# The expert products of the first block, reordered: eight by the high weights, then four by the low weights behind a wait of their own

## The reference, cut to what matters

```
logits = u @ router_w + router_b ; top 4 of 32 experts per token, softmax gates
for each block of gathered token rows xb of an expert e:
    gu  = xb @ w_gu[e] + b_gu[e]                    # 1024 -> 2048
    act = (clip(up) + 1) * gate * sigmoid(1.702 * gate)
    out = act @ w_down[e] + b_down[e]               # 1024 -> 1024
h += gate-weighted sum of the experts' outputs ; final RMSNorm
```

## Time and profile before

| what | value |
|---|---|
| time, median of 3 runs | 2208.36 us (2207.04 to 2212.03) |
| the profiled execution, its own time | 2210.34 us |
| its span, first to last instruction | 2208.3 us |
| mean granted TensorE clock over the span | 0.978 |
| expert stage, about | 650 to 2180 us of the span |

### The profile page before, as it was taken

How to read it: one execution, slowest core, us unless ns; L and a number is a source line. 1 busy time by engine, 2 the same in 40 slices (tenths; PEclk the granted TensorE clock), 3 DMA queues, 4 the chain that set the end, 5 groups by cost and what they waited for, 6 DMA issues and landing times. The chain is left out here.

```text
span 2208.3 us, 35903 instructions
## 1 busy us (share of the span) xinstructions
PE 2133.2 (97%) x11230; PEld 1811.5 (82%) x11231; DVE 1706.5 (77%) x2127; ACT 1373.6 (62%) x1752; POOL 408.2 (18%) x436
## 2 busy tenths in 40 slices
PE   7999999988959999999999999999999999999998
PEld 7987777767848998898898898988889998889884
DVE  5426667776658777979979978779997778998897
ACT  4324655544447566757857757567775667776675
POOL 0000000002342121213213213212321222221120
PEclk9999999999969999999999999999999999999996
DMA  4111101207859776979979979669997769998897
GB/s 162 44 48 34 58 34 44 101 31 229 181 185 343 248 241 248 377 265 349 382 263 353 377 259 352 236 243 380 373 382 267 252 229 332 388 364 336 290 370 283
DMA packets 106797, 548.41 MB, mean 248 GB/s; under 512 B 18071, under 2 KB 28824, under 8 KB 51834
## 3 DMA queue, kind: packets, MB, share of 16 engines
q1 hardware_dynamic: 88138, 504.89, 61.2%
q0 software_dynamic: 18608, 42.85, 8.1%
HBM read 516.45 MB, written 41.47 MB: 253 GB/s over the span
## 5 line engine op out<-in xcount | busy, mean ns | idle before, releaser
L2431 DVE TENSOR_TENSOR wl<-raw,wh 128x2048 fp32r<-128x2048 f32 x423 | 959.1, 2287 | 44.0 <-PE sums L2188 26.8
L2292 ACT ACTIVATE wh<-raw 128x2048 fp32r<-128x2048 f32 x425 | 804.7, 1912 | 113.2 <-PE sums L2188 39.4
L2172 PE MATMUL sums<-wh,xx 128*128 128x512 f32 x832 | 325.8, 392 | 0.9 <-issue 0.9
L2171 PE MATMUL sums<-wl,xx 128*128 128x512 f32 x832 | 325.6, 391 | 0.0
L2170 PE MATMUL sums<-wh,xx 128*128 128x512 f32 x832 | 325.3, 391 | 0.0
L2103 POOL DMA_INDIRECT h_dram<-y,pairs_mine x47 | 120.8, 2570 | 769.1 <-DVE y L2525 449.2
L2170 PE MATMUL sums<-wh,al 128*128 128x512 f32 x560 | 226.7, 405 | 0.6 <-DVE al L2516 0.3
L2172 PE MATMUL sums<-wh,ah 128*128 128x512 f32 x560 | 219.1, 391 | 0.0
L2171 PE MATMUL sums<-wl,ah 128*128 128x512 f32 x560 | 218.5, 390 | 0.0
L2171 PEld LDWEIGHTS sums<-wl,xx 128*128 128x128 f32 x832 | 156.9, 189 | 34.0
L2172 PEld LDWEIGHTS sums<-wh,xx 128*128 128x128 f32 x832 | 156.7, 188 | 33.4
(11 more groups left out here) (402 smaller groups left out, 4174.6 us busy)
## 6 DMA issues: line engine op xcount, KB each, us to landing
raw<-in_w_experts SPq DMA_DIRECT2D x426, 1024.0 KB, 6.5
raw<-in_w_chan SPq DMA_DIRECT2D x20, 512.0 KB, 3.3
o_gate<-in_x SPq DMA_DIRECT2D x8, 512.0 KB, 5.9
raw<-in_w_out SPq DMA_DIRECT2D x8, 512.0 KB, 5.5
ht<-in_x SPq DMA_DIRECT2D x8, 512.0 KB, 5.9
h_dram<-ht SPq DMA_DIRECT2D x8, 512.0 KB, 9.0
u_dram<-ut SPq DMA_DIRECT2D x8, 512.0 KB, 10.1
h_all<-h_dram SPq DMA_DIRECT2D x8, 512.0 KB, 6.8
```

The lines of the kernel that those rows point to most:

```text
L2171: pe.matmul(out, hi[:, n, :], w_lo[:, kk, :], start=False, stop=False)
L2172: last = pe.matmul(out, hi[:, n, :], w_hi[:, kk, :], start=False, stop=half == 1 and kk == 3)
L2292: nc.scalar.activation(wh[ch % HIGHS][:, :, :], raw[ch % RAW][:, :, :], ACT.Copy).then_inc(h_split.sem, 1)
L2431: dve.tensor_tensor(wl[ch % LOWS][:, :, :], raw[ch % RAW][:, :, :], wh[ch % HIGHS][:, :, :], ALU.subtract).then_inc(l_split.sem, 1)
```

## The change

Only `first_block` changes. Before, the chunk waits for its low weights and runs, for each of its four tiles, the three matmuls in turn. After, it waits at its head for its high weights only, runs the two matmuls by the high weights of all four tiles (eight in all), waits for its low weights, and runs the four matmuls by the low weights. The wait for the activations stays in the first loop, in front of tiles n = 4 and n = 6 of chunk 10. The number of matmuls, their operands and the chunk's last signal stay.

```
     def first_block(i, ch):
         g, half = GROUP_OF[ch], HALF_OF[ch]
-        pe.wait_ge(*low_done(i, ch))
+        pe.wait_ge(h_split.sem, h_split.at(i, ch + 1))
...
             if ch == LAST_CHUNK[4] and n % 2 == 0:
                 pe.wait_ge(a_low.sem, a_low.at(i, n // 2 + 1))
             pe.matmul(out, lo[:, n, :], w_hi[:, kk, :], start=g >= 4 and n == 0, stop=False)
-            pe.matmul(out, hi[:, n, :], w_lo[:, kk, :], start=False, stop=False)
-            last = pe.matmul(out, hi[:, n, :], w_hi[:, kk, :], start=False, stop=half == 1 and kk == 3)
+            pe.matmul(out, hi[:, n, :], w_hi[:, kk, :], start=False, stop=False)
+        pe.wait_ge(*low_done(i, ch))
+        for kk in range(4):
+            n = half * 4 + kk
+            last = pe.matmul(out, hi[:, n, :], w_lo[:, kk, :], start=False, stop=half == 1 and kk == 3)
         return last
```

## The result

Over 22 runs of each kernel the median went from 2209.74 us (2205.71 to 2212.03) to 2211.37 us (2209.21 to 2217.18). The ratio is 1.0014, with a 95% interval from 1.0008 to 1.0020: 3.1 us slower (1.8 to 4.4). The two medians are only 1.6 us apart; the means, 2209.29 and 2212.36 us, are 3.1 apart, because five of the runs after lie above 2214 us and none of those before does. It is slower, but within the 0.2% that the prediction called no change; forecast were 6.2 us.

What follows compares the result with a forecast made beforehand. PE was taken to bound the kernel, busy for 1491.5 of 1495 us of the expert stage. Chunk 10's stalls of 4.6, 0.4 and 1.2 us sum to 6.2, so 2208.4 becomes 2214.6 us, range 2209.3 to 2218.3.

Steps and rivals of the forecast that it cites:

- Starting on the high weights gains nothing.: At the head of each chunk: the wait for low weights never held PE, so moving it back gains 0 us.
- The added waits and the operand order are free.: In all 348 `first_block` calls: one more satisfied wait and another operand order, both taken as 0 us.
- the 3.5 us at the top of the range: Upper bound for the 348 added waits at 0.01 us each; a little of it was put into the range's top.
- The fourth pair is due two products earlier, and a typical single item loses 0.27 us.: Chunk 10, single items: the fourth activation pair is awaited before product five, not seven; 17 items lose 0.27 us each.
- The item that the sum took at 0.43: One single item whose fourth pair in chunk 10 is 0.16 us later than in the typical ones; loss 0.43 us.
- The five late items.: Five single items where chunk 10's load already waited for `al` before, 2.5 us in total; forecast to add 1.2 us.
- A wait in the chain is a wait of the whole stage, since PE has no idle time later in which to make it good.: Expert stage: PE's stalls in chunk 10 were counted in full towards the kernel's time, 6.2 us.
- the likeliest case: The stall in chunk 10, chance 0.72: 6.2 us slower, 2214.6 us.
- the case in which nothing measurable happens: Rival, chance 0.18: PE's loads run far enough ahead, or something else paces the item; 2208.4 us, give or take 1.
- The step of 216 ns: The skill's spacing of 512-column matmuls, against 226 to 230 ns in the rows; would make the sum about 0.6 us smaller.
- The rival of something else being the pacer: Single items paced by something other than PE, above all DMA at share 0.99; 2208.4 us, within a chance of 0.18.
- The rival of a faster kernel by earlier sequencing: Second matmul after transposes starts 0.08 us sooner at 139 places, 11 us less the 6.2: 2203.5 us, chance 0.04.

## Why the prediction was right or wrong

**Starting on the high weights gains nothing.** Right: no row after waits for `wl`, and the kernel with all chunks but chunk 10 reordered is as fast as before.

**The added waits and the operand order are free.** Right within what the times can tell; 1392 extra waits cost some 0.5 us in their trace, so the 3.5 us at the top of the range were not needed.

**The fourth pair is due two products earlier, and a typical single item loses 0.27 us.** Right in place, number and size: 23 waits, 11.2 us (forecast 10 to 12), 0.25 to 0.28 us in chunk 10 of 21 of the 23 items. The item that the sum took at 0.43 was one of them, at 0.27.

**The five late items.** Taken as +1.2 us between -0.35 and 2.3. Chunk 10 took 5.6 us more in all, of which the 18 others account for 18 x 0.27 = 4.9, so the five cost 0.7. Only two were late after. Whether PE's delays let DMA catch up, as I argued, or whether it was chance, one execution of each can't say. Between the three traces with the new order and the four with the old one, chunk 10 differs by 7.2 us on average; less the 4.9 that leaves 2.3, the upper bound. So the 1.2 is neither confirmed nor excluded, and what makes these items late stays open.

**"A wait in the chain is a wait of the whole stage, since PE has no idle time later in which to make it good."** This is the step that failed. PE did have idle time later, 0.20 us at 14 passages from a single item to a single one, in front of the biases. It is worth 2.8 us, nearly the whole difference between the 6.2 us forecast and the 3.1 measured. The row that shows it was in hand, second in the earlier trace rows: PEld's L2158 waits for ACT's `y`, 14 times, 4.9 us. Two readings hid it. The windows showed PE busy for 35.76 of 35.76 us, although 0.2 us of it was standing. Matmuls overlap: around the biases the starts are 0.32 and 0.34 us apart instead of 0.23 (1896.60, 1896.92, 1897.26), and durations of 0.39 and 0.50 us cover both. And 4.9 us was read as one of the small waits that exist, not as slack that a later PE would eat. One such wait, listed at 0.35 us, is a load 0.32 late, which costs 0.32 - 0.12 = 0.20 us. The Trainium skill warns of the first reading in "Perfetto Trace Analysis", section "Identifying the Most-Contended Engine": the busy share of matmuls is not a good measure of how close a kernel is to its roofline. The rows here agree that it hides time, 35.76 of 35.76 busy with a wait in it that the kernel with `y` copied sooner takes out. The reason that the section gives, pipelined instructions that look smaller in the trace, is another one than here, where durations of 0.39 us lie over steps of 0.23.

What the sum should have been: where the next item is single (15 passages, 14 of them waiting), 0.27 - 0.20 = 0.07 us; where it is a two-block item, or the stage's end, the whole 0.27. That is 6.2 - 14 x 0.20 = 3.4 us.

**The forecast and its range.** The chances put 0.71 on slower by more than 0.2% and 0.25 on within it; the second came. The range of 2209.3 to 2218.3 us holds the 2211.37 measured, but the likeliest case's own range, 2211.5 to 2217.5, doesn't: it was held by the part that was added for the case in which nothing measurable happens. The start was off as well, by chance of three runs: 2208.4 us, where the 22 runs before have a median of 2209.7.

**The step of 216 ns.** The section that the prediction cites from the Trainium skill, "Back-to-back issue gap" in "TensorE: Matmul & The Clock Gate", calls the 216 ns the gap of an isolated matmul, and gives 131 ns for a stream of weight loads and matmuls of 512 columns. The rows here show 226 to 230 ns for such a stream. Neither figure fits, and the sum rightly goes by the trace.

**The rival of something else being the pacer** was named with DMA. The engine that gave time back was ACT, and only in part; the right form of the rival was a second wait behind the first.

**The rival of a faster kernel by earlier sequencing** did not happen: the second matmul after transposes still starts 0.31 us after the first (1893.04 to 1893.35 after).

## What to carry to other kernels

When a change makes the bounding engine stand somewhere, list its other waits in the same loop before multiplying: each one behind the new stall, whose releaser does not move with it, takes up to what it costs back (here 0.20 us, which its list shows as 0.35). A reordering by one operand's readiness moves the due time of every other operand in the list; write down for each wait how many instructions stand in front of it before and after. And where a tight operand is found, the cheap edit is to ask for it last: here that, with the second wait removed as well, made the kernel 6.2 us faster than before.

## What the runs showed of the hardware that was not expected

A matmul's weight load that comes late, counted from the start of the product before it, costs its lateness less 0.12 us: 0.39 late cost 0.27 in the kernel after, and the loads for `al`, `ah` and the biases that came 0.24 to 1.0 us late in the stages of the ten traces, 138 of them, all cost their lateness less 0.10 to 0.12. The 0.12 us belong to a load in the middle of a stream: the load of the first product behind the transposes, 1.26 us late with the wait at the chunk's head, cost 1.26 us. The waiting load starts 0.05 to 0.06 us after the end of `al` in the middle of the stream, and 0.11 to 0.12 behind the transposes (1911.03 to 1911.15 above).

A satisfied wait in front of a matmul costs nothing that the times would show with 1392 of them (ratio 0.9996, 0.9987 to 1.0005). In the trace it costs 0.08 us at 6 places, all behind a load that had stalled, and nothing in the middle of a stream, where the steps stay at 0.23 us.
